# Twenty-four attention units projected in pairs by seven products in the gate stage, and read back as rows in the attention stage

## The reference

```python
xn = rmsnorm(x, norm_pre)
z = einsum('bld,dn->bln', xn, w_in)              # 1024 -> 13312 columns
aq, ak, av, ag, bq, bfg, bi, bg, cu, cg, mg = split_in(z)
# A: 3 groups of heads (window, dilation) = (128,1), (512,4), (2048,16), 4 heads x 128 each;
#    softmax attention in each group, the three outputs weighted by softmax over their log-sums
o_a = einsum('gblh,gblhe->blhe', softmax(lses), outs);  y_a = o_a * silu(ag)
# B: gated linear recurrence, 8 heads;  C: causal pooling, 4 groups
gates = sigmoid(mg.reshape(b, L, 3, D_MODEL))
merged = gates[0]*(y_a @ w_br_a) + gates[1]*(y_b @ w_br_b) + gates[2]*(y_c @ w_br_c)
x_next = x + rmsnorm(merged @ w_out, norm_post)
```

## Time and profile before

| what | value |
|---|---|
| three runs | 1889.86, 1890.29, 1890.33 us (median 1890.29) |
| profiled execution | 1890.18 us, its span 1888.4 us |
| PE busy | 1855.9 us, 98% of the span, 13888 matmuls |
| DVE, ACT, POOL busy | 823.6, 388.6, 523.1 us |
| granted TensorE clock, mean | 0.997 of full speed |
| transfers | 176.14 MB, mean 93 GB/s |

### The profile page before, as it was taken

One profiled execution on the slowest core, in us unless ns is written; L12 is line 12 of the kernel. 1 busy time (PEld: TensorE's weight loads), 2 busy tenths in 40 slices (PEclk: granted clock), 3 DMA queues, 4 the chain that ended last, 5 costly groups with the idle time before them and its releaser, 6 DMA issues. The chain is left out here.

```text
span 1888.4 us, 34540 instructions
## 1 busy us (share of the span) xinstructions
PE 1855.9 (98%) x13888; PEld 1783.9 (94%) x13888; DVE 823.6 (44%) x1390; ACT 388.6 (21%) x929; POOL 523.1 (28%) x354
## 2 busy tenths in 40 slices
PE   7999999999999999999999999999999999999998
PEld 6999999999999999999999999999999999999997
DVE  8723311331231233124175576566466375426623
ACT  6322222211221221221101101101101123213321
POOL 1466643212212221221221122112212233336400
PEclk9999999999999999999999999999999999999999
DMA  5332224243143233414211111112202134656622
GB/s 168 113 106 93 93 92 119 53 111 109 47 96 97 78 64 100 114 44 98 85 46 58 46 56 58 58 44 69 63 28 70 36 118 157 205 168 220 186 76 89
DMA packets 245169, 176.14 MB, mean 93 GB/s; under 512 B 35789, under 2 KB 226637, under 8 KB 245068
## 3 DMA queue, kind: packets, MB, share of 16 engines
q1 hardware_dynamic: 205036, 132.51, 24.8%
q10 hardware_dynamic: 40032, 42.15, 6.4%
HBM read 131.83 MB, written 42.79 MB: 92 GB/s over the span
## 5 line engine op out<-in xcount | busy, mean ns | idle before, releaser
L236 PE MATMUL psum<-x_hi,w_hi 128*128 128x384 f32 (+1 forms) x2208 | 728.5, 335 | 6.2 <-PEq L129 3.8
L236 PE MATMUL psum<-x_lo,w_hi 128*128 128x384 f32 (+1 forms) x2208 | 712.2, 327 | 0.0
L207 POOL CAST w_hi<-w_raw 128x1024 fp32r<-128x1024 f32 (+1 forms) x108 | 120.5, 1116 | 1139.2 <-PE psum L236 883.9
L236 PEld LDWEIGHTS psum<-x_hi,w_hi 128*128 128x128 f32 x2208 | 415.9, 188 | 19.9 <-issue 13.9
L236 PEld LDWEIGHTS psum<-x_lo,w_hi 128*128 128x128 f32 x2208 | 416.4, 189 | 0.0
L236 PE MATMUL psum<-x_hi,w_lo 128*128 128x384 f32 (+1 forms) x2208 | 412.0, 326 | 0.0
L236 PEld LDWEIGHTS psum<-x_hi,w_lo 128*128 128x128 f32 x2208 | 370.5, 188 | 0.0
L209 POOL TENSOR_TENSOR w_lo<-w_raw,w_hi 128x1024 fp32r<-128x1024 f32 (+1 forms) x108 | 262.5, 2430 | 8.6
L2081 ACT ACTIVATE a_feature<-psum 128x384 f32<-128x384 f32 (+1 forms) x100 | 45.2, 452 | 349.6 <-PE psum L236 349.6
L2193 DVE TENSOR_TENSOR a_prob<-psum,band 128x128 f32<-128x128 f32 (+1 forms) x64 | 21.5, 378 | 200.1 <-PE psum L1887 198.9
L1399 PEld LDWEIGHTS psum<-b_q_decayed,b_k_decayed 128*64 128x64 f32 x1584 | 51.3, 138 | 12.9 <-issue 8.4
(11 more groups left out here) (284 smaller groups left out, 2503.9 us busy)
## 6 DMA issues: line engine op xcount, KB each, us to landing
w_raw<-in_w_in SPq DMA_DIRECT2D x94, 512.0 KB, 4.0
gate_rows<-x_rows ACTq DMA_DIRECT2D x20, 544.0 KB, 2.7
s_cached<-in_cache_kv_w SPq DMA_DIRECT2D x128, 64.0 KB, 2.5
s_cached<-in_cache_kv_w SPq DMA_DIRECT2D x64, 128.0 KB, 2.4
spare<-branch_outputs SPq DMA_DIRECT2D x13, 544.0 KB, 6.2
a_feature<-group_weights SPq DMA_DIRECT2D x12, 512.0 KB, 5.8
c_gate<-gate_rows SPq DMA_DIRECT2D x11, 544.0 KB, 4.8
c_gate_raw<-gate_rows SPq DMA_DIRECT2D x11, 544.0 KB, 4.0
```

The source lines that it names most:

```text
L207: pool.tensor_copy(w_hi[:, s, 0:nko, :], w_raw[:, s, 0:nko, :]).then_inc(self.hi_ready, 1)
L236: mm = pe.matmul(psum[:, c, 0:n], w[:, s, k, :], x[:, k, t0:t0 + n], start=step is first, stop=step is last)
```

## The change

The gate stage gets twelve more pairs (`PAIRS` = 22, of which `GATE_PAIRS` = 10 are the old ones). They are, for all four heads, the queries and keys of groups two and three, the values of group one, and the gate: six units a head, twenty-four in all. Their rows go to DRAM as the gates' do, 46 rows in place of 22; they get no sigmoid there, and DVE and ACT write them regrouped by class (`add`, `by_class`, `in_order`). A part that reaches into the sample tokens takes one more DVE instruction.

The attention stage keeps four units a head: 0, 1, 7 and 8. The other six come by one transfer of 544 KB each from `gate_rows` straight into their tiles (`row`, `row_in`); ACT only copies their sample parts (`sample_of`) and applies the sigmoid to the gate in one instruction. SP's list for a head is written anew, and so are the places of the chunks in PE's list.

```diff
-            PAIRS = 10
+            GATE_PAIRS, PAIRS = 10, 22
             HK, HN, N = KO // 2, NT // 2, NT // 4
             ORDER = (0, 3, 1, 2, 5, 4, 6)
-            SHIFT = 66
+            SHIFT = 7 * PAIRS - 4
...
+                ROWS = ((COL_AQ + GROUP, 1), (COL_AK + GROUP, 1), (COL_AQ + 2 * GROUP, 2), (COL_AK + 2 * GROUP, 2), (COL_AV, 0), (COL_AG, 0),)
...
+                def in_order(n, x, w):
+
+                    step = (1, 4, 8)[ROWS[(n - GATE_PAIRS) // 2][1]] if n >= GATE_PAIRS else 1
+                    return x[:, 0:w].rearrange("p (m r) -> p r m", r=step)
...
+                            if n < GATE_PAIRS:
+                                at = COL_MG + (D + 4 * P + 2 * P * n if n < 2 else
+                                               2 * P * (n - 2) if n < 6 else 2 * D + 2 * P * (n - 6))
+                            else:
+                                at = ROWS[(n - GATE_PAIRS) // 2][0] + (n - GATE_PAIRS) % 2 * 2 * P
                             for u in range(2):
                                 sp.dma_start(raw[n % 2][:, u, :, :], col(w_in, at + u * P)).then_inc(raw_in[n % 2], 16)
...
+                        def add(dst, t0, n, r, j, kept):
+                            if n < GATE_PAIRS:
+                                ins = dve.tensor_tensor(dst[:, t0:t0 + N], bank(n, r, j), kept, ALU.add)
+                            else:
+                                w = min(N, SEQ - t0)
+                                ins = dve.tensor_tensor(by_class(n, dst, t0, t0 + w), in_order(n, bank(n, r, j), w),
+                                                        in_order(n, kept, w), ALU.add)
+                                if w < N:
+                                    ins = dve.tensor_tensor(dst[:, SEQ:NT], bank(n, r, j)[:, w:N], kept[:, w:N], ALU.add)
+                            ins.then_inc(summed, 1)
...
-            UNITS, MISC = 10, 48
+            UNITS, MISC = 4, 48
...
+                FROM_ROWS = (2, 3, 4, 5, 6, 9)
+                HERE = [j for j in range(len(COLS)) if j not in FROM_ROWS]
+                AT = {j: n for n, j in enumerate(HERE)}
+                sample_ready = sem("a_sample_ready", scope)
+                gate_ready = sem("a_gate_ready", scope)
+                row_in = {j: sem(f"a_row_in{j}", scope) for j in FROM_ROWS}
...
-                            for j in range(SLOTS, UNITS):
-                                cv.load(sp, h * UNITS + j, j % 2, col(w_in, h * P + COLS[j]))
-                                if j == 4:
-                                    sp.wait_ge(s_o_done, h + 1)
-                                    sp.sem_inc(cv.held_sp, 1)
-                                if j in (4, 5):
-                                    for b in range(4 * (j - 4), 4 * (j - 4) + 4):
-                                        load_rows(sp, kv[b], b, 0, hd, k_in[b])
-                                if j == 6:
-                                    for b in range(4):
-                                        load_rows(sp, kv[VC[b]], b, 1, hd, v_in[b])
+                            def keys_in(half):
+                                for b in range(4 * half, 4 * half + 4):
+                                    load_rows(sp, kv[b], b, 0, hd, k_in[b])
+
+                            def row(j, dst=None):
+                                dst = DST[j] if dst is None else dst
+                                sp.dma_start(dst[:, :], gates_d[bass.ds(h + (22 + AH * FROM_ROWS.index(j)), 1), :, :]
+                                             .rearrange("o p t -> p (o t)")).then_inc(row_in[j], 16)
+
+                            def weights(j):
+                                cv.load(sp, h * UNITS + AT[j], AT[j] % 2, col(w_in, h * P + COLS[j]))
+
+                            sp.wait_ge(y_ready, h + 1)
+                            sp.sem_inc(cv.held_sp, 1)
+                            row(2)
+                            row(3)
+                            sp.wait_ge(scores_max, h * AG + 1)
+                            sp.sem_inc(cv.held_sp, 1)
+                            row(4)
+                            sp.wait_ge(krow_ready, h * 6 + 1)
+                            sp.sem_inc(cv.held_sp, 1)
+                            row(5)
+                            weights(7)
+                            sp.wait_ge(s_o_done, h + 1)
+                            sp.sem_inc(cv.held_sp, 1)
+                            keys_in(0)
+                            keys_in(1)
+                            sp.wait_ge(scores_max, h * AG + 2)
+                            sp.sem_inc(cv.held_sp, 1)
+                            row(6)
+                            weights(8)
+                            sp.wait_ge(y_out, h * 16 + 16)
+                            sp.sem_inc(cv.held_sp, 1)
+                            row(9, graw)
+                            for b in range(4):
+                                load_rows(sp, kv[VC[b]], b, 1, hd, v_in[b])
                             cv.load(sp, h * UNITS + UNITS, 0, after[0])
...
                             unit(1)
-                            unit(2)
                             scores(0)
                             k_rows(0)
-                            unit(3)
-                            unit(4)
+                            chunk(7, 0)
+                            pe.wait_ge(sample_ready, 2 * h + 1)
                             scores(1)
                             k_rows(1)
-                            unit(5)
-                            unit(6)
+                            chunk(7, 1)
+                            pe.wait_ge(sample_ready, 2 * h + 2)
                             scores(2)
                             k_rows(2)
...
-                            chunk(7, 0)
                             keys_t(0)
                             keys_t(1)
-                            chunk(7, 1)
+                            chunk(7, 2)
                             pe.wait_ge(y_ready, h + 1)
                             key_scores(0)
                             keys_t(2)
                             keys_t(3)
-                            chunk(7, 2)
                             key_scores(2).then_inc(keys_used, 1)
                             keys_t(4)
                             keys_t(5)
                             mm.then_inc(cv.misc_done, 1)
                             chunk(8, 2)
                             v_rows(1)
-                            unit(9)
+                            next_head(0)
...
                             turn(0)
                             sample_values()
-                            chunk(UNITS, 0)
                             sample_back()
                             for n in range(1, N_PT):
                                 turn(n)
                                 values(n - 1)
                             values(N_PT - 1).then_inc(o_done, 1)
-                            chunk(UNITS, 1)
-                            chunk(UNITS, 2)
+                            next_head(1)
+                            next_head(2)
...
+                            def sample_of(j):
+                                act.wait_ge(row_in[j], h * 16 + 16)
+                                new = DST[j][:, SEQ:NT]
+                                if j in U_Q:
+                                    g = U_Q.index(j)
+                                    own_queries(g, new)
+                                    return act.activation(qh[:, g, :], new, ACT.Copy)
+                                return act.activation(kh[:, U_K.index(j), :], new, ACT.Copy)
...
                             chunk(0, 2)
                             unit(1)
-                            unit(2)
-                            unit(3)
+                            sample_of(2)
+                            sample_of(3).then_inc(sample_ready, 1)
                             exps(0)
                             act.wait_ge(krow_ready, h * 6 + 1)
                             rows_out(0, 0, krow, krow_out)
-                            unit(4)
-                            unit(5)
+                            sample_of(4)
+                            sample_of(5).then_inc(sample_ready, 1)
                             exps(1)
                             act.wait_ge(krow_ready, h * 6 + 2)
                             rows_out(1, 0, krow, krow_out)
-                            unit(6)
                             chunk(7, 0)
+                            chunk(7, 1)
                             exps(2)
-                            chunk(7, 1)
                             chunk(7, 2)
...
-                            for c in range(NCH):
-                                cv.empty(act, u + U_G, c, gate, ACT.Sigmoid, raw=graw)
+                            act.wait_ge(row_in[U_G], h * 16 + 16)
+                            act.activation(gate[:, :], graw[:, :], ACT.Sigmoid).then_inc(gate_ready, 1)
```

65 lines of the change are left out of this document (40 added, 25 removed).

## The result

The changed kernel takes 1978.2 us (median of 5 runs, 1976.4 to 1983.3), the kernel before 1889.9 us (5 runs beside them): 1.0477 times as long, with an interval of 1.0466 to 1.0488, or +88.3 us. Forecast were 1950 us in a range up to 1975. The direction and the places were right; the sum was too small by 28 us, and 1978.2 lies outside the range.

What follows compares the result with a forecast made beforehand. PE, busy 98% of the span, was taken as the bound. Four heads with 23.0 us of new waits each (92.0) less 32.4 saved gave +59.6 on 1890.2, rounded 1950 us; range 1910 to 1975.

Steps and rivals of the forecast that it cites:

- (e): Wait ahead of `sample_back` for the chain of small transfers ending with the spread group weights: 5.0 us a head, ends 0 and 9.
- (c): Start of unit 7's chunk 0, behind the idle stretch: matmuls at a low clock, 1.7 us a head, ends 0 and 4.2.
- (b): PE's wait behind `k_rows(0)` for unit 7's weights, requested late by SP: 12.7 us a head, ends 9.4 and 14.
- Pairs: Gate stage: twelve pairs at 21.02 us each in place of twenty-four units at 23.72 a two save 32.4 us.
- (a): `scores(0)`, now directly behind unit 1, waits until ACT has emptied the last chunk: 0.7 us a head.
- rival 3: Longer waits: sums and group weights queue behind 2 MB of other transfers, clock low behind both waits: 1980 us, chance 0.13.
- (d): Behind `scores(2)`, waits for DVE's copies at `keys_t` and `key_scores(2)`: 2.9 us a head, ends 1.5 and 4.
- A: Start of unit 7's chunk 0, forecast 36.4 us after PE's chunk 1 of unit 0.

Runs made afterwards that it cites:

- e4: The change's twelve extra pairs kept, but the attention stage given back its six units a head as in the kernel before: 2141.8 us, 1.1336.
- e3: The changed kernel with 66 unused matmuls of 384 columns put into the wait ahead of unit 7: 1966.6 us, 1.0412.
- e2: The changed kernel with group two's key rows in tiles of their own, so DVE needn't wait for their store: 1980.2 us, 1.0477.
- e6: The changed kernel with all 24 value loads issued on SP behind the group weights: 2008.4 us, 1.0624.
- e1: The changed kernel with unit 7's weights requested by SP at the head's start, not behind two waits on DVE: 1957.2 us, 1.0359.
- e9: The changed kernel's head reordered: weights and key loads early, value loads split around the sums, PE's chunks among scores and key work, separate key-row tiles: 1904.0 us, 1.0069.
- e12: e9 with group two's exponentials earlier, some value loads on ACT, group weights before value rows on DVE, next head's second weights before the spread: 1912.4 us, 1.0118.

## Why the prediction was wrong

Two steps failed: the chain (e), from the start of unit 7 to `sample_back`, was summed 4.3 us too short, and the clock (c) was priced in one place at 1.7 us. The waits' places and the largest of them, (b), were right. Point by point:

- **Pairs**: 32.4 us saved, right (e4 and the 252.2 us).
- **(a)** 0.7 forecast, 0.64 measured.
- **(b)** 12.7 forecast; 13.7 in the second head, 51.8 / 4 = 12.9 on the mean. The request stood at 28.75 us for 28.2. Right, with its reasons.
- **(c)** failed as a size. One cold chunk at 1.7 was priced. It was 7.1 - 4.2 = 2.9 in the second head and 2.5, 1.8 and 2.5 in the others, 2.4 on the mean (e3 took nearly all of it away). And the value loop behind `sample_back` took 3.0 us more than 13.1 in two of the four heads, which is on the path: 1.5 a head on the mean. The text had the thought that would have given it, that the head pays behind (b) and behind (e), and set it aside: the second was in rival 3 alone. A third place, behind the wait at `keys_t`, was not seen at all: 5.0 us for 3.5 in the second head. It lies ahead of a later wait for the chain.
- **(d)** 2.9 forecast, 27.3 / 4 = 6.8 measured, since DVE also waited for the store of group two's key rows, which was not seen. That part cost nothing (e2): PE would have waited for the chain later.
- **(e)** the chain was the right one, its sum too short. In the second head, from A: the sums are issued at +23.4 (forecast 22.5); the load that brings them back goes out after 9.6 us (7.37), the group weights after 8.2 (8.94), the spread loads after 17.8 (16.79), `sample_back` after 5.8 (5.0): +4.2 in all. On the mean of four heads the steps are 23.0, 9.3, 8.9, 17.8 and 5.8, and the whole is 64.9 us for 60.6. The largest part, 2 us, is the way of the sums to DRAM. In the kernel before SP requested nothing in the 6 us ahead of them; here it requested 12 value loads and 512 KB of weights. e6 took the 12 loads away and had 7.6 us in place of 9.6. For the other parts no run shows the cause: the group weights have 12 value loads right ahead of them in both kernels.

As a chain in the second head: A was 1.4 us late, `sample_back` 4.2 more, the value loop 3.1 more: 8.6 us on 110.1, a head of 118.7. On the mean they are 0.6, 4.3 and 1.5: a head of 116.6, and 4 x 6.5 = 26 of the 28 us (the profiled execution took 1976.4). Added up along PE the same is seen from the other side: the five places cost 92.8 / 4 = 23.2 us a head for 21.3 forecast without the clock, and all that is left, 6.4 us a head for 1.7, is nearly all slow matmuls. (e) read as PE's idle time was only 2.8 for 5.0, and (d) 6.8 for 2.9: what (c) and (d) take, (e) no longer shows. That the sum along PE was not further off is so in part luck.

Rival 3, longer waits, gave 1980 us, and its two reasons were there: the sums travelled longer behind the value loads, and the clock was low behind both waits (behind the second in two heads of four). But its number is luck too: it had 14, 3.5 and 9 us for (b), (d) and (e), where 12.9, 6.8 and 2.8 were measured. The prediction also says that before the change the chain had ended long before `turn(0)`. In the second head the first spread load went out at 558.00 and took 4.0 at least to land, and `turn(0)` stood at 565.7: 3 to 4 us, not long.

**Why half of the work gone brings no gain.** From the first sum's issue to the spread's issue the second heads have 33.1 us before, 35.6 after, 35.8 in e1, 36.5 in e9, 39.9 in e12 and 45.4 in e6: no order made it shorter. In e9 the exponentials end 39.1 us into the head, `sample_back` follows 43.7 later, and the loop takes 15.4: 98.2. To beat the kernel before, the four heads would have to be under 87.0 + 8.1 = 95.1 us. (Not all of e9's 14 us lie in the heads: behind the last, PE waits 5.3 us at the start of branch B, for 1.1 before.) The units that left a head had been this chain's cover: in the kernel before, PE came to `sample_back` 48.8 us behind the last exponential. None of the versions run beats the kernel before; a shorter form of the transfers themselves (group weights not in 4-byte pieces) was not tried.

## What to carry to other kernels

Before work is taken out from between a chain's start and its end, add up the chain: in none of these orders was a head shorter than its hidden transfers and the list that SP works off ahead of them. Price a wait twice, as idle time and as slow matmuls behind it, the second with a range: here it came behind every long wait, and behind the short one in two heads of four. And when one wait is removed, take as the gain only what the next event on the chain allows: in e1 13 us a head of waiting went, and the head became 5 us shorter.

## What the runs showed of the hardware

- The granted clock was 0.57 in the 7.1 us from the start of the chunk behind a wait of 13.7 us, and 0.50 behind one of 2.8 us with a loosely filled stretch ahead. A value loop of 13.1 us took 16.2 and 16.1 us behind waits of 2.80 and 3.19 us, and 13.2 behind 2.44 and 2.73.
- The sums go to DRAM in two stores of 8 KB. The load that brings them back goes out 7.4 us after the first store in the kernel before, 9.6 in the change, 8.9 in e9 and 12.2 in e12 (second heads).
- The group weights, 12 KB in 4-byte pieces, hold the spread back for 16.8 us in the kernel before, where the DMA engines are busy for 0.16 of the last 14.6 us of that, and for 17.8 to 21.3 us in the change, e9 and e12. The Trainium skill ("DMA: Bandwidth & Descriptors", Rules for kernel authors) says that a last dimension that isn't contiguous becomes one descriptor an element. The profile agrees: from 543.40 to 558.00 SP's queue has 1691 packets there for 0.01 MB.
- Single loads behind such pieces held SP for up to 3.66 us in e6's second head, where most took 0.4 to 0.6. The cause isn't shown.
